# Gate products by seven block products for half of the row tiles, and branch rounds in another order

## The chip, the cores and the metric

One Trainium2 chip, one of its cores. The metric is device time in microseconds (us) of one execution, lower is better. Engines: TensorE (PE) for matmuls, VectorE (DVE), ScalarE (ACT), GpSimd (POOL), and SyncE (SP), which issues most DMAs; each works through its own list in order, and they meet through semaphores.

## What is computed

One decoder layer on 256 tokens, all in float32 (the reference, cut):

```python
h = rms_norm(x, g_attn[l])
qa, ka, va, fa, qb, kb, vb, ga, gb = jnp.split(h @ w_in[l], offs, axis=-1)
o_a = merge_heads(fox_attention(q_a, k_a, v_a, log_f))          # 8 heads, forgetting
o_b = merge_heads(dilated_attention(q_b, k_b, v_b, slopes))     # 8 heads, dilated
merged = jax.nn.sigmoid(ga) * (o_a @ w_br_fox[l]) + jax.nn.sigmoid(gb) * (o_b @ w_br_dil[l])
x = x + merged @ w_out[l]
u = rms_norm(x, g_ffn[l]) @ w_up[l]        # 2048 -> 2 x 5632, causal conv over 3 tokens
x = x + (jax.nn.silu(gate) * val) @ w_down[l]
```

The width is 2048; the gates ga and gb are 2048 columns each.

## The kernel before

Every product is float32 made of three passes in fp32r: activations and weights are split into a high and a low part, and high x high, high x low and low x high are summed in a PSUM bank. Tokens are two row tiles of 128. A weight tile is 256 rows of the contraction by 512 columns (512 KB). One such tile is a **unit**: ACT writes its high part (`high(n)`, w_hi), DVE its low part (`low(n)`, w_lo), PE runs 2 row tiles x 2 contraction tiles x 3 passes = 12 matmuls over it (`rows_unit`) and counts up `used`. w_hi and w_lo are rings of RING = 6 units: `high(n)` waits for unit n - 6 to be used, so ACT and DVE work up to six units ahead of PE. Raw weights go through 4 slots of `raw` (SP loads a slot again once `low` has read it).

A round is 8 units: one block of 512 columns over all of the contraction. The order is: 12 rounds for queries, keys and values in 4 groups of 4 heads (a slot is a unit's place in its group, 0 to 23); 8 gate rounds (ga and gb by turns for the column blocks c = 0 to 3), each evacuated by ACT with a sigmoid; 4 branch rounds, of which units 0 to 3 are the forgetting half into banks 0 and 1 and units 4 to 7 the dilated half into banks 2 and 3; the output rounds; then the feed-forward part. Attention of a group runs between the units of the next group: scores, softmax on DVE and ACT (`softmax_head`, `exps`), transposes of the probabilities (`copy_pt`), values, and the split of the output (`out_high`, `out_low`) into actB. The last four heads (12 to 15) run between the units of the gate rounds, at u = 1, 4 and 7 of the ga rounds. `fox_part` and `dil_part` multiply branch banks by the gates; the sum in `tmp` is transposed after unit 2 of the next round and split into actA (`merged_high`, `merged_low`, which counts `mt_lo`).

The feed-forward part already multiplies half of the contraction of each pair of up blocks by seven block products instead of eight (P1 to P7). A product unit has one row tile: 6 matmuls. The weights of P7, P6, P5 and P4 are sums of tiles; they are made in place in raw_x and raw_y (two tiles each) by accumulating DMAs that POOL issues (`add_tile`) and by adds on DVE, while SP loads the plain tiles. Sums of banks are made by ACT copies and DVE adds. The order is written out by hand on each engine; waits are on constant counts.

## Time and profile before

| | us |
|---|---|
| median of 3 runs | 1385.45 (1384.43 to 1386.55) |
| the profiled execution, its own time | 1384.28 |
| its span, first to last instruction | 1382.5 |
| PE busy | 1371.6 (99%) |
| DVE, ACT, POOL busy | 969.0, 776.6, 94.7 |
| DMA, whole span | 290.52 MB, 210 GB/s |

An engine's busy time is the union of its instructions. Matmuls overlap in the pipeline, so a matmul's own duration is longer than its spacing. "Idle before" is the time in which the engine waited for the named releaser. The stages in this execution: group 3 of the heads from 241 us, gate rounds 307.0 to 484.7, branch rounds to 575, output rounds and the start of the feed-forward part after that; a steady feed-forward block is 64.4 us, as 755.5 to 819.9.

### The profile page before, as it was taken

To read this page: it belongs to the slowest core of one execution; us is meant where nothing else is said; L and a number is where in the kernel's file an instruction comes from. 1 tells how busy PE (TensorE), PEld (TensorE's weight loads), DVE (VectorE), ACT (ScalarE), POOL (GpSimd) and SP (SyncE) were. 2 spreads that over 40 slices of the span, in tenths; PEclk is the share of its full clock that TensorE was granted. 3 is DMA by queue.
4 is the path that set the end of the run, shared out by engine and by line. 5 is a ranking of instruction groups with operands and counts; after the bars stand their busy time and mean duration, and the time that the engine had idled before them with its cause. 6 is when DMAs were issued, how large, how long until landed. Compare 5 with 4: busy or idle time off the path is not lost.

```text
span 1382.5 us, 16197 instructions
## 1 busy us (share of the span) xinstructions
PE 1371.6 (99%) x6241; PEld 1136.2 (82%) x6241; DVE 969.0 (70%) x1196; ACT 776.6 (56%) x963; POOL 94.7 (7%) x115
## 2 busy tenths in 40 slices
PE   9999999999999999999989999999999999999999
PEld 7888888888888888888878888888888888888887
DVE  5646555665554456657688979788878888797975
ACT  6655455454545444446675656565665666565652
POOL 0101011100000000001010101010010101010100
PEclk9999999999999999999999999999999999999999
DMA  9765555556666555667898787696878787878741
GB/s 337 242 207 170 171 168 168 175 165 185 181 192 186 187 192 183 218 226 220 272 245 264 206 249 229 197 267 181 270 182 286 170 290 181 267 203 248 224 139 61
DMA packets 112189, 290.52 MB, mean 210 GB/s; under 512 B 11368, under 2 KB 12656, under 8 KB 111600
## 3 DMA queue, kind: packets, MB, share of 16 engines
q1 hardware_dynamic: 98528, 250.83, 54.3%
q0 software_dynamic: 9504, 34.61, 14.0%
q10 hardware_dynamic: 4080, 4.05, 0.9%
q8 instruction: 49, 0.80, 0.2%
q14 instruction: 28, 0.23, 0.1%
HBM read 287.34 MB, written 2.11 MB: 209 GB/s over the span
## 4 chain that ended last, share of the span: by engine, by line
PE 97%; DMA 1%; DVE 1%; ACT 0%; issue 0%; SPq 0%; POOL 0%; ACTq 0%
PE acc L430 21%; PE acc L432 20%; PE acc L431 20%; PE acc L448 6%; PE acc L452 6%; PE acc L450 6%; PE acc L463 5%; PE acc L467 5%; PE acc L465 5%; PE acc L654 1%; DMA raw_y<-w_up 1%; PE acc L488 1%; PE acc L476 1%; PE acc L496 1%; PE acc L509 0%; DVE w_lo L1111 0%
## 5 line engine op out<-in xcount | busy, mean ns | idle before, releaser
L1111 DVE TENSOR_TENSOR w_lo<-raw,w_hi 128x1024 fp32r<-128x1024 f32 x291 | 354.0, 1224 | 267.5 <-ACT w_hi L791 265.3
L791 ACT ACTIVATE w_hi<-raw 128x1024 fp32r<-128x1024 f32 x291 | 307.4, 1059 | 318.8 <-PE acc L432 272.3
L430 PE MATMUL acc<-w_hi,actA 128*128 128x512 f32 x1116 | 442.4, 396 | 1.4 <-DVE w_lo L1111 1.4
L432 PE MATMUL acc<-w_hi,actA 128*128 128x512 f32 x1116 | 435.1, 390 | 0.0
L431 PE MATMUL acc<-w_lo,actA 128*128 128x512 f32 x1116 | 434.4, 389 | 0.0
L432 PEld LDWEIGHTS acc<-w_hi,actA 128*128 128x128 f32 x1116 | 209.5, 188 | 44.5
L430 PEld LDWEIGHTS acc<-w_hi,actA 128*128 128x128 f32 x1116 | 209.7, 188 | 43.7 <-issue 2.0
L431 PEld LDWEIGHTS acc<-w_lo,actA 128*128 128x128 f32 x1116 | 209.8, 188 | 41.9
L448 PE MATMUL acc<-w_hi,actB 128*128 128x512 f32 x352 | 137.1, 390 | 0.0
L452 PE MATMUL acc<-w_hi,actB 128*128 128x512 f32 x352 | 137.0, 389 | 0.0
L450 PE MATMUL acc<-w_lo,actB 128*128 128x512 f32 x352 | 136.9, 389 | 0.0
L791 ACT ACTIVATE w_hi<-raw_y 128x1024 fp32r<-128x1024 f32 x88 | 93.2, 1060 | 68.7 <-PE acc L432 32.4
L1111 DVE TENSOR_TENSOR w_lo<-raw_y,w_hi 128x1024 fp32r<-128x1024 f32 x88 | 107.3, 1222 | 31.9 <-ACT w_hi L791 31.8
L791 ACT ACTIVATE w_hi<-raw_x 128x1024 fp32r<-128x1024 f32 x66 | 70.0, 1061 | 53.7 <-PE acc L452 32.6
L1111 DVE TENSOR_TENSOR w_lo<-raw_x,w_hi 128x1024 fp32r<-128x1024 f32 x66 | 78.9, 1219 | 9.0 <-ACT w_hi L791 9.0
L1542 POOL DMA_DIRECT2D raw_y<-w_up x44 | 38.4, 872 | 642.1 <-DVE w_lo L1111 598.8
L452 PEld LDWEIGHTS acc<-w_hi,actB 128*128 128x128 f32 x352 | 66.1, 188 | 13.9
L450 PEld LDWEIGHTS acc<-w_lo,actB 128*128 128x128 f32 x352 | 66.1, 188 | 13.8
L448 PEld LDWEIGHTS acc<-w_hi,actB 128*128 128x128 f32 x352 | 66.1, 188 | 13.7
L1371 DVE SCALAR_TENSOR_TENSOR work<-acc,smalls_sb,work 128x255 f32<-128x255 f32 (+1 forms) x176 | 72.5, 474 | 0.6 <-ACT work L1008 0.6
L463 PE MATMUL acc<-w_hi,actB 128*128 128x512 f32 x176 | 69.4, 394 | 0.0
L1404 DVE TENSOR_TENSOR work<-acc,work 128x512 f32<-128x512 f32 x88 | 56.6, 684 | 17.6 <-PE acc L432 17.6
(179 smaller groups left out, 1579.5 us busy)
## 6 DMA issues: line engine op xcount, KB each, us to landing
raw<-w_in SPq DMA_DIRECT2D x159, 512.0 KB, 3.8
raw_x<-w_up SPq DMA_DIRECT2D x44, 512.0 KB, 5.0
raw_y<-w_up POOLq DMA_DIRECT2D x44, 512.0 KB, 7.9
raw<-w_up SPq DMA_DIRECT2D x38, 512.0 KB, 4.6
raw<-w_down SPq DMA_DIRECT2D x34, 512.0 KB, 5.0
raw<-w_out SPq DMA_DIRECT2D x28, 512.0 KB, 4.1
raw_y<-w_up SPq DMA_DIRECT2D x22, 512.0 KB, 4.2
raw_x<-w_up POOLq DMA_DIRECT2D x22, 512.0 KB, 5.5
```

The lines of the kernel that those rows point to most:

```text
L430: nc.tensor.matmul(o, lhsT=a_h, rhs=w_hi[:, s, k, :], start=first and k == 0, stop=False)
L431: nc.tensor.matmul(o, lhsT=a_h, rhs=w_lo[:, s, k, :], start=False, stop=False)
L432: mm = nc.tensor.matmul(o, lhsT=a_l, rhs=w_hi[:, s, k, :], start=False, stop=last and k == KU - 1)
L448: nc.tensor.matmul(o, lhsT=a_h, rhs=w_hi[:, s, k, :], start=False, stop=False, skip_group_check=True)
L450: nc.tensor.matmul(o, lhsT=a_h, rhs=w_lo[:, s, k, :], start=False, stop=False, skip_group_check=True)
L452: mm = nc.tensor.matmul(o, lhsT=a_l, rhs=w_hi[:, s, k, :], start=False, stop=kt == KT - 1, skip_group_check=True)
L463: nc.tensor.matmul(o, lhsT=a_h, rhs=w_hi[:, s, k, :], start=first and kt == 0, stop=False, skip_group_check=True)
L465: nc.tensor.matmul(o, lhsT=a_h, rhs=w_lo[:, s, k, :], start=False, stop=False, skip_group_check=True)
L467: mm = nc.tensor.matmul(o, lhsT=a_l, rhs=w_hi[:, s, k, :], start=False, stop=kt == HK - 1, skip_group_check=True)
L791: nc.scalar.activation(w_hi[:, n % RING, :, :], src.rearrange("p (k n) -> p k n", k=KU), ACT.Copy).then_inc(hi_done, 1)
L1111: nc.vector.tensor_tensor(w_lo[:, n % RING, :, :], src.rearrange("p (k n) -> p k n", k=KU), w_hi[:, n % RING, :, :].bitcast(f32), ALU.subt ...
L1371: t = nc.vector.scalar_tensor_tensor(out=conv[:, j, lag:SEQ], in0=bank[(4, 7)[j // 2]][:, (j % 2) * SEQ:(j % 2 + 1) * SEQ - lag], scalar=s ...
```

## The change

For each column block c the ga and gb rounds are done together. The first 1024 of the 2048 rows of the contraction are done by seven products (P3, P1, P7, P6, P5, P2, P4, each 2 units of 6 matmuls), the other 1024 in the plain form (4 units for ga, 4 for gb, 12 matmuls each), in the order of `gate_units`. The four quarters of the activations are rebuilt from their high and low parts by DVE in slots 8 to 11 of group 3 (`quarters`), their differences formed in slots 12 to 15 and split by ACT (slots 14, 16, 17, 19, 20) and DVE (18 to 21). The parts of P3, P5 and P6 lie in actB[10:16], so the outputs of heads 10 and 11 are kept in `kept` and split later (`kept_lo`). The weights' sums are made in raw_x and raw_y as in the up blocks: POOL's accumulating DMA after P3's split (into raw_y) and after P7's t2 add (into raw_x), DVE adds after P7 (t2) and P2 (t4); there is no accumulate for P4. ACT copies bank 0 after P1, P6, P5 and the last plain unit, DVE adds banks 7, first, 3, second and 7 again into ga and gb; the sigmoids follow in place, two wide ones for each c, those of c during block c + 1, the last in branch round 0. The four gate banks are given out by `gate_banks`.

The branch rounds have 4 units each: the four forgetting ones first, then the four dilated ones; banks (1, 3) and (0, 2) by turns. Heads 12 to 15 move from the gate rounds to the forgetting rounds: scores after unit 0, transposes of the probabilities after unit 3, values after unit 0 of the next round (head 15: of the first dilated round). The merged block is transposed after unit 2 of the next dilated round. Output rounds use banks (6, 7), (1, 3), (0, 2); in the first feed-forward block it is P1 that waits for x2_done 3, where the next output unit did. On SP the raw_x and raw_y loads of the gates stand between the plain ones; on POOL prepare_dil of heads 13 to 15 comes after the gates' accumulates.

```diff
+
+        units += product("P3") + plain(0, 0) + product("P1") + plain(0, 1) + product("P7")
+        units += product("P6") + plain(0, 2) + product("P5") + plain(0, 3) + plain(1, 0)
+        units += product("P2") + plain(1, 1) + product("P4") + plain(1, 2) + plain(1, 3)
...
+
+OUT_BANKS = ((6, 7), (1, 3), (0, 2))
 
 
 def ffn_units():
...
+        def gate_part(name, kt):
+            if name in GATE_PARTS:
+                part = parts_g[:, GATE_PARTS.index(name), kt, :]
+                return part[:, 0:P], part[:, P:2 * P]
+            at, r = {"P1": (kt, 0), "P7": (kt, 1), "P2": (HK + kt, 0), "P4": (HK + kt, 1)}[name]
+            return actA[:, at, r * P:r * P + P], actA[:, at, SEQ + r * P:SEQ + r * P + P]
...
+                    continue
+                _, c, name, q = unit
+                if name == "P5":
+                    sp.wait_ge(lo_done, n)
+                    load_gate_b21(c, q)
+                elif name == "P2" and c < 3:
+                    sp.wait_ge(t4_added, QU * c + q + 1)
+                    load_gate_b11(c + 1, q)
+                elif name == "P4" and c < 3:
+                    sp.wait_ge(lo_done, n)
+                    load_gate_b22(c + 1, q)
...
+            def gate_product(n, c, name, q):
+
+                first_bank, second_bank = gate_banks(c)
+                if q == 0:
+                    if c == 0:
+                        pe.wait_ge(h_part_lo, 4 if name == "P7" else 3)
+                        pe.wait_ge(h_part_hi, 3 if name == "P3" else 6)
+                    if name == "P3" and c:
+                        pe.wait_ge(g_c11, c)
+                    elif name == "P1" and c:
+                        pe.wait_ge(g_u1, c)
+                    elif name == "P7" and c:
+                        pe.wait_ge(g_c22, c)
+                        pe.wait_ge(g_c21, c)
+                    elif name == "P7":
+                        pe.wait_ge(qkt_done, 4 * GROUPS)
+                    elif name == "P6":
+                        pe.wait_ge(g_p1, c + 1)
+                    elif name == "P5":
+                        pe.wait_ge(g_v, c + 1)
+                o = bank[{"P3": second_bank, "P1": 0, "P7": 7, "P6": 0, "P5": 0, "P2": first_bank, "P4": 3}[name]]
+                pe.wait_ge(lo_done, n)
+                s = n % RING
...
+            def gate_plain(n, c, side, j):
+
+                first_bank, second_bank = gate_banks(c)
+                if side == 0 and j == 0 and c:
+                    pe.wait_ge(g_c12, c)
+                    pe.wait_ge(g_c21, c)
+                elif side == 0 and j == 0:
+                    pe.wait_ge(act_evac, 4)
+                pe.wait_ge(lo_done, n)
+                s = n % RING
+                for r, o in enumerate((bank[second_bank], bank[0]) if side else (bank[first_bank], bank[3])):
+                    if side and r and j == 0:
+                        pe.wait_ge(g_u0, c + 1)
...
-                for m in range(2):
-                    R = GATE0 + m + 2 * c
-                    pe.wait_ge(act_evac, 3 + m + 2 * c)
-                    for u in range(UPR):
-                        rows_unit(UPR * R + u, actA, (KU * u, KU * u + 1), bank[2 * m:2 * m + 2], u == 0, u == UPR - 1)
-                        if m == 0 and u == 1:
-                            attend_scores(q_of(3)[:, c, :], lambda a, b: k_of(3)[:, c, a:b])
-                        elif m == 0 and u == 4:
-                            attend_transpose(12 + c)
-                        elif m == 0 and u == 7:
-                            v = v_of(3)
-                            attend_values(12 + c, v[:, 0, c * P:(c + 1) * P], v[:, 1, c * P:(c + 1) * P])
...
+                if c == 0:
+                    pe.wait_ge(g_c11, 4)
+                    pe.wait_ge(g_c21, 4)
+                elif c == 1:
+                    pe.wait_ge(g_u1, 4)
+                    pe.wait_ge(g_c12, 4)
+                else:
+                    pe.wait_ge(fox_merged, c - 1)
+                for u in range(4):
+                    branch_unit(c, u)
+                    if u == 0:
+                        if c:
+                            last_values(c - 1)
+                        attend_scores(q_of(3)[:, c, :], lambda a, b: k_of(3)[:, c, a:b])
+                    elif u == 3:
+                        attend_transpose(12 + c)
...
                 if c == 0:
-                    pe.wait_ge(fox_merged, 4)
+                    pe.wait_ge(g_c22, 4)
                     pe.wait_ge(mt_lo, 6)
                 elif c == 1:
...
+                        if g == 3 and slot in (14, 16, 17):
+                            name = {14: "P5", 16: "P6", 17: "P3"}[slot]
+                            act.wait_ge(h_made, {"P5": 5, "P6": 7, "P3": 8}[name])
+                            nc.scalar.activation(parts_g[:, GATE_PARTS.index(name), :, 0:P],
+                                                 h_of[{"P5": 2, "P6": 0, "P3": 3}[name]], ACT.Copy)\
+                                .then_inc(h_part_hi, 1)
...
+                if unit == ("H", c, "P1", QU - 1):
+                    act.wait_ge(used, n + 1)
+                    nc.scalar.activation(ga[:, 0, to], bank[0], ACT.Copy, scale=-1.0).then_inc(g_p1, 1)
+                elif unit == ("H", c, "P6", QU - 1):
+                    act.wait_ge(used, n + 1)
+                    nc.scalar.activation(ga[:, 1, to], bank[0], ACT.Copy, scale=-1.0).then_inc(g_v, 1)
+                elif unit == ("H", c, "P5", QU - 1):
+                    act.wait_ge(used, n + 1)
+                    if c == 0:
+                        act.wait_ge(h_part_lo, 4)
+                    nc.scalar.activation(gb[:, 0, to], bank[0], ACT.Copy).then_inc(g_u0, 1)
+                elif unit == ("G", c, 1, PLAIN - 1):
+                    act.wait_ge(used, n + 1)
+                    if c == 3:
+                        act.wait_ge(kept_lo, 1)
+                    nc.scalar.activation(gb[:, 1, to], bank[0], ACT.Copy).then_inc(g_u1, 1)
...
+            def gate_sigmoid(c):
+                act.wait_ge(g_c11, c + 1)
+                act.wait_ge(g_c12, c + 1)
+                act.wait_ge(g_c21, c + 1)
+                act.wait_ge(g_c22, c + 1)
+                for r in range(RT):
+                    both = work_rows[:, :, r, c * NB:(c + 1) * NB]
+                    nc.scalar.activation(both, both, ACT.Sigmoid, scale=xrs[:, r:r + 1]).then_inc(g_sig, 1)
...
+                for u in range(4):
+                    high(BR_UNIT + 4 * c + u + RING)
+                    if u == 0:
+                        if c:
+                            out_high(12 + c - 1)
+                        exps(12 + c)
+                    elif u == 1 and c == 0:
+                        gate_sigmoid(3)
+                    elif u == 3:
+                        copy_pt(12 + c)
...
+            def gate_bank_sums(n, unit):
+
+                c = unit[1]
+                first_bank, second_bank = gate_banks(c)
+                to = slice(c * NB, c * NB + NB)
+                if unit == ("H", c, "P3", 0) and c:
+                    before = slice(c * NB - NB, c * NB)
+                    dve.wait_ge(g_u1, c)
+                    gate_rest(gb[:, 1, before])
+                elif unit == ("G", c, 0, 2):
+                    dve.wait_ge(g_v, c + 1)
+                    gate_result(bank[7], ga[:, 1, to], g_v7)
+                elif unit == ("H", c, "P2", QU - 1):
+                    dve.wait_ge(used, n + 1)
+                    dve.wait_ge(g_p1, c + 1)
+                    gate_result(bank[first_bank], ga[:, 0, to], g_c11)
+                elif unit == ("H", c, "P4", QU - 1):
+                    dve.wait_ge(used, n + 1)
+                    dve.wait_ge(g_v7, c + 1)
+                    gate_result(bank[3], ga[:, 1, to], g_c21)
+                elif unit == ("G", c, 1, PLAIN - 1):
+                    dve.wait_ge(used, n + 1)
+                    dve.wait_ge(g_u0, c + 1)
+                    gate_result(bank[second_bank], gb[:, 0, to], g_c12)
...
             def fox_part(c):
-                dve.wait_ge(used, UPR * (BR0 + c) + 4)
+                dve.wait_ge(used, BR_UNIT + 4 * c + 4)
+                dve.wait_ge(g_sig, 2 * c + 2)
                 for r in range(RT):
-                    t = nc.vector.tensor_tensor(tmp[:, r, :], bank[r][:, :], ga[:, r, c * NB:(c + 1) * NB], ALU.mult)
+                    part = ga[:, r, c * NB:(c + 1) * NB]
+                    t = nc.vector.tensor_tensor(part, bank[br_banks(c)[r]], part, ALU.mult)
...
+            for n, unit in enumerate(GATES, GATE_UNIT):
+                _, c, kind, q = unit
+                if kind == "P3":
+                    pool.wait_ge(lo_done, n)
+                    add_gate_tile(c, q, raw_y[:, q, :], y_summed[q])
+                elif kind == "P7":
+                    pool.wait_ge(t2_added, QU * c + q + 1)
+                    add_gate_tile(c, q, raw_x[:, q, :], x_summed[q])
             for c in range(1, 4):
```

## Rows read from the trace of the kernel before

**Rows 1.** The page: busy us, share of span, count; granted clock in tenths by 40 slices.

```profile
PE 1371.6 (99%) x6241; PEld 1136.2 (82%) x6241; DVE 969.0 (70%) x1196; ACT 776.6 (56%) x963; POOL 94.7 (7%) x115
PEclk9999999999999999999999999999999999999999
```

**Rows 2.** Waits of PE: engine, line waited for, us in total, times, longest.

```profile
PE acc L654 <- DVE tmp L1414: 3.0, 1, 3.0
PE acc L463 <- ACT tmp L1038: 1.5, 1, 1.5
```

**Rows 3.** Windows: busy us and count by engine, clock, DMA share, GB/s.

```profile
core 0: us, PE busy (x) PEld busy (x) DVE busy (x) ACT busy (x) POOL busy (x), PEclk, DMA share, GB/s
...
307.00:484.70 177.70, 177.70 (x799) 147.41 (x798) 88.48 (x111) 89.51 (x108) 3.04 (x6) 1.00 0.63 186
...
755.50:819.90 64.40, 64.40 (x293) 53.48 (x292) 54.02 (x64) 39.57 (x44) 5.23 (x7) 1.00 0.79 229
```

**Rows 4.** PE's timeline in a gate round: start, duration, two units' first matmuls.

```profile
339.28 0.39 PE L430 MATMUL acc<-w_hi,actA 128*128 128x512 f32 x1
...
342.00 0.39 PE L430 MATMUL acc<-w_hi,actA 128*128 128x512 f32 x1
```

**Rows 5.** Timelines of ACT and DVE there: one unit's high and low part.

```profile
343.62 1.06 ACT L791 ACTIVATE w_hi<-raw 128x1024 fp32r<-128x1024 f32 x1 [1.66 <-PE acc L432]
...
344.71 1.23 DVE L1111 TENSOR_TENSOR w_lo<-raw,w_hi 128x1024 fp32r<-128x1024 f32 x1 [1.50 <-ACT w_hi L791]
```

**Rows 6.** DVE's timeline in a steady feed-forward block: bank sums; t2 add.

```profile
828.04 1.29 DVE L1404 TENSOR_TENSOR work<-acc,work 128x512 f32<-128x512 f32 x2 [0.34 <-PE acc L432]
...
834.54 1.22 DVE L1115 TENSOR_TENSOR raw_y<-raw_y,raw_x 128x1024 f32<-128x1024 f32 x1
```

**Rows 7.** POOL's accumulates issued in 690:700, 730:760 and 760:790: issue to landing.

```profile
DMA to landing us min/median/max: 9.4/10.7/12.0
...
DMA to landing us min/median/max: 5.4/5.4/5.5
...
DMA to landing us min/median/max: 5.4/7.1/10.9
```

**Rows 8.** The page's DMA issues: count, KB each, median us to landing.

```profile
raw<-w_in SPq DMA_DIRECT2D x159, 512.0 KB, 3.8
raw_x<-w_up SPq DMA_DIRECT2D x44, 512.0 KB, 5.0
...
raw_y<-w_up SPq DMA_DIRECT2D x22, 512.0 KB, 4.2
```

**Rows 9.** DMA queues in 307:484, then in 719:1300: packets, MB, share.

```profile
q1 hardware_dynamic: 17002, 32.79, 62.2%
...
q1 hardware_dynamic: 28288, 103.04, 50.4%
q0 software_dynamic: 7980, 29.06, 28.1%
```

**Rows 10.** POOL's timeline: prepare_dil of head 12.

```profile
294.05 0.83 POOL L1506 TENSOR_TENSOR softmax<-consts_sb,st 128x384 f32<-128x384 f32 x1
```

**Rows 11.** A head's softmax on DVE, and the table loads that ACT does.

```profile
356.73 0.55 DVE L1123 TENSOR_TENSOR softmax<-acc,softmax 128x384 f32<-128x384 f32 x1
...
360.07 0.55 DVE L1147 TENSOR_SCALAR softmax<-softmax,st 128x128 f32<-128x128 f32 x2
...
373.21 1.28 ACT L969 ACT_TABLE_LOAD   x1
374.51 1.27 ACT L969 ACTIVATE work<-acc,st 128x512 f32<-128x512 f32 x2
```

**Rows 12.** Branch round 1 on PE and DVE: transposes of the merged block, their split.

```profile
514.46 1.03 PE L476 MATMUL acc<-smalls_sb,tmp 128*128 128x128 f32 x8
515.25 0.48 PE L430 MATMUL acc<-w_hi,actB 128*128 128x512 f32 x1
...
515.81 1.23 DVE L1111 TENSOR_TENSOR w_lo<-raw,w_hi 128x1024 fp32r<-128x1024 f32 x1 [1.20 <-ACT w_hi L791]
...
520.56 1.28 DVE L1159 TENSOR_TENSOR actA<-acc,actA 128x512 fp32r<-128x512 f32 x2
```

More of the change, by code:

```diff
@@ new lines, in _, with branch_unit @@
+            pe.wait_ge(qn_done, 2 * GROUPS)
+            for n, unit in enumerate(GATES, GATE_UNIT):
+                if unit[0] == "H":
+                    gate_product(n, unit[1], unit[2], unit[3])
+                else:
+                    gate_plain(n, unit[1], unit[2], unit[3])
+            def branch_unit(m, u):
+                pair = [bank[b] for b in br_banks(m)]
+                kt = KU * u if m < 4 else KT // 2 + KU * u
+                rows_unit(BR_UNIT + 4 * m + u, actB, (kt, kt + 1), pair, u == 0, u == 3)
@@ L806, in out_high @@
                 act.wait_ge(o_ready, h + 1)
-                nc.scalar.activation(actB[:, h, 0:SEQ], bank[6][:, 0:SEQ], ACT.Copy).then_inc(o_hi, 1)
+                if h in (10, 11):
+                    nc.scalar.activation(kept[:, h - 10, :], bank[6][:, 0:SEQ], ACT.Copy).then_inc(o_lo, 1)
+                else:
+                    nc.scalar.activation(actB[:, h, 0:SEQ], bank[6][:, 0:SEQ], ACT.Copy).then_inc(o_hi, 1)
             def merged_high(c):
@@ L974, in _, with gate_sum @@
-            for c in range(4):
-                for u in range(UPR):
-                    high(UPR * (BR0 + c) + u + RING)
-                    if c and u == 2:
+            def gate_sum(n, unit):
+                c = unit[1]
[16 more added lines that the diff above has]
+                    nc.scalar.activation(gb[:, 1, to], bank[0], ACT.Copy).then_inc(g_u1, 1)
@@ new lines, in gate_sigmoid @@
+            def gate_sigmoid(c):
[6 more added lines that the diff above has]
+                    nc.scalar.activation(both, both, ACT.Sigmoid, scale=xrs[:, r:r + 1]).then_inc(g_sig, 1)
+            for n, unit in enumerate(GATES, GATE_UNIT):
+                gate_sum(n, unit)
+                high(n + RING)
+                _, c, kind, j = unit
+                if unit == ("G", c, 0, 1):
+                    if c:
+                        gate_sigmoid(c - 1)
+                    if c == 3:
+                        act.wait_ge(used, GATE_UNIT + GATES.index(("H", 3, "P3", QU - 1)) + 1)
+                        nc.scalar.activation(actB[:, 10:12, 0:SEQ], kept, ACT.Copy).then_inc(kept_hi, 1)
@@ L1249, in _ @@
                             softmax_head(h, prep, g == 3)
-                        elif g > 0 and at == 5:
+                        elif g > 0 and at == 5 and h < 10:
                             out_low(h)
+                        if g == 3:
+                            quarters(slot)
                         if u == (UPR - 1 if R else UPR - 2) and m < 2:
@@ L1315, in _ @@
+                nc.vector.tensor_tensor(tmp[:, :, :], ga[:, :, c * NB:(c + 1) * NB], gb[:, :, c * NB:(c + 1) * NB],
+                                        ALU.add).then_inc(merged, 1)
             for c in range(4):
-                for u in range(UPR):
-                    low(UPR * (BR0 + c) + u + RING)
+                for u in range(4):
+                    if c == 0 and u == 0:
+                        dve.wait_ge(g_u1, 4)
+                        gate_rest(gb[:, 1, 3 * NB:4 * NB])
+                    elif u == 3:
+                        fox_part(c)
+                    low(BR_UNIT + 4 * c + u + RING)
+                    if u == 0:
+                        if c:
+                            out_low(12 + c - 1)
+                        dve.wait_ge(prep_ready, prepared(12 + c))
+                        softmax_head(12 + c, prep, True)
@@ L1318, in _ @@
+            for c in range(4):
+                for u in range(4):
                     if u == 3:
@@ L1321, in _ @@
                             dve.wait_ge(mt_ready, 2 * c)
-                        else:
-                            dve.wait_ge(act_evac, 4 + 8)
-                        fox_part(c)
-                dil_part(c)
+                        dil_part(c)
+                    low(BR_UNIT + 16 + 4 * c + u + RING)
+                    if c == 0 and u == 0:
+                        out_low(15)
             def add_x2(n, c, banks):
```

326 lines of the change are left out of this document (244 added, 82 removed).

## Prediction, made before the change was run

> **What bounds the kernel now.** I read the page first, then the waits of PE, then the windows by stage, and only then single rows. The page shows TensorE busy for 1371.6 of 1382.5 us at the full granted clock of 2.4 GHz, with no slice below it [rows 1]. PE's waits say where it was not busy: besides the first microseconds, 3.0 and 1.5 us in the first feed-forward block [rows 2], and nothing in the stages that this change touches. In the gates' stage (307.0 to 484.7 us) PE is busy for the whole of its 177.7 us while DVE is busy for 88.5, ACT for 89.5 and the DMA engines at 0.63 [rows 3]. So PE is the bound there, and only matmuls less, or a new wait on PE, move the end.
>
> **What one matmul costs.** A matmul's row says 0.39 us, but that is latency in a pipeline. Two first matmuls of following units start at 339.28 and 342.00 us, twelve matmuls apart [rows 4]: 2.72 / 12 = 0.2267 us each. It is the same in product units: a feed-forward block issues 276 long matmuls and 16 transposes (two groups of some 0.9 us) and takes 64.4 us [rows 3]; 276 x 0.2267 = 62.6. A change of weights or bank costs no extra. So a plain unit (two row tiles) takes 2.72 us and a product unit (one row tile of products, 6 matmuls) 1.36.
>
> **1. Gates by seven products.** Before: 4 column blocks x 2 gates x 8 units x 12 = 768 matmuls. After, for each c: 7 products x 2 units x 6 = 84, and 8 plain units x 12 = 96, together 180; 720 in all. Removed: 48 x 0.2267 = **10.9 us**, all on the path. A block now takes 180 x 0.2267 = 40.8 us.
>
> **2. What the other engines get for it.** Units grow from 64 to 88. Each is split by ACT (1.06 us) and DVE (1.23 us), and DVE's comes out about 2.35 us after ACT may start [rows 5]. For each block DVE has 22 x 1.23 = 27.1, four adds of whole tiles (t2, t4) at 1.22 = 4.9, five sums out of banks at 0.64 = 3.2 [rows 6]: 35.2 of 40.8 us. ACT has 22 x 1.06, four copies of a bank (0.6 each) and two wide sigmoids (1.1 each): 28. Both fit, DVE at 86%. They run six units ahead of PE, so what is late in a stretch of products (1.36 us a unit on PE, 2.45 on DVE for P7 with its add) is caught up in plain units (2.72). Cost taken: nothing. If that cover were gone, DVE's 35.2 us still lies under 40.8.
>
> The PE waits on banks are each covered by work in between: P6 after P1's copy by one plain and two product units (5.4 us against 0.6), P5 after P6's by one plain unit (2.7 against 0.6), the second row tile of G10 after P5's by 4.1, the next block's P1 after the last copy by 5.4. Where they are thinnest, 2 us remain.
>
> **3. The loop through the buffers.** raw_x and raw_y go round: P3 split, accumulate (D), P7 split, t2, accumulate (D), P5 split, load into raw_x, P2 split, t4, P4 split, load into raw_y, next P3. In numbers: five splits of 2.35, two adds of 1.25, 2.5 of queue on DVE and ACT before P4 (its neighbours' splits, t4 of the other half and P5's copy), loads of 5.0 and 4.2 [rows 8], so 25.95 + 2D. POOL's accumulates land 5.4 to 5.5 us after issue when two are alone, up to 10.9 when four queue up in one product stretch, and 9.4 and 12.0 beside SP's burst of loads in the first block [rows 7]. The gates queue never more than two and have no such burst. With D = 5.5 the loop is 36.95 us, under the block's 40.8, and PE waits for nothing; it closes at D = 7.4. Walking the units one by one, the split of the tightest ones (P5, P6, P7) ends 5 us before PE comes to them, so a late transfer first eats 5 us. With three returns the stall is about 3 x (2D - 14.9) - 5 us: none to D = 8.2, 7 at 9.5, 10.4 at 10, 22 at 12.
>
> What D is for w_in no row shows: its rows are 2 KB, those of w_up here 4 KB. From above: a software packet takes 28.1% x 16 x 581 / 7980 = 0.33 us in the feed-forward stage [rows 9]; an accumulate of w_up is 145 packets, 2.9 us of all engines. A tile of w_in is some 274 packets; if each still took 0.33, that were 5.6 us and D 8.2 alone, 12 for the second of a pair. From below: plain loads of w_in take 62.2% x 16 x 177 / 17002 = 0.104 us a packet against 50.4% x 16 x 581 / 28288 = 0.166 for w_up, so half the row is nearly half the time (18% more by the byte), and land after 3.8 us, not later than w_up's [rows 8, 9]. That excludes a gain but gives D = 5.4 to 6. I take 6, since the plain loads are the same rows of the same tensor; both ends stay in the range. The engines' load goes from 0.63 to about (14 x 1.77 + 4 x 3.4) / 40.8 = 0.94 by the packets' times under light load, 0.85 if they shorten as in other full stretches: high, so D is the weak number.
>
> The Trainium skill (DMA: Bandwidth & Descriptors, "Why small descriptors are slow") gives a fixed cost of about 3 cycles per packet beside one cycle per 32 bytes. By that, 2 KB rows would cost 2% more than 4 KB rows, not the 18% that the queue's rows show here; D would be 5.5 and the sum the same.
>
> **4. First block and the quarters.** In group 3 DVE gets 12 operations of about 0.65 and ACT six of 0.6 (four quarters rebuilt, four differences, splits). DVE is busy 0.6 of the time in that stage and idles 1.5 us in most slots [rows 5], so they go into gaps. PE's P3 needs those of slot 20, ready more than 5 us before. POOL's first accumulate stands behind prepare_dil(12), which ends at 294.9 us [rows 10]; it lands by 302 to 307, P7's split could start at 308.4. Nothing.
>
> **5. Last four heads in the forgetting rounds.** The attention matmuls and transposes are as many as before: 0. Their chain gets tighter, 4 units a round. Scores to normalised took 356.73 to 360.6 us = 3.9 [rows 11], 2.3 after the unit's end; with out_low (0.4) before it, ready 6.7 us after the unit that issues the scores, against three units = 8.2 until the transposes. DVE per round: 4 x 1.23 + 3.9 + 0.4 + 1.3 (fox_part) = 10.5 of 11.8. The one tight place is round 0: ACT has gate_sigmoid(3) between exps(12) and copy_pt(12): a table load of 1.28 [rows 11] and 2.1 of sigmoid, then two late splits. By addition copy_pt is ready 11.75 us after the first unit; PE wants it at 4 x 2.72 + 0.8 = 11.7. Cost: 0 to 0.3.
>
> The rows show one table load, 1.28 us, and the next activation starts 0.01 after it. The Trainium skill (ScalarE: Activation LUTs, "What ACT_TABLE_LOAD costs") adds a drain to about 2.66 us a switch; the rows do not show it. With it round 0 would wait 1.4 us more.
>
> **6. Dilated rounds of 4 units.** Transposes after unit 2 now leave one unit (2.72) before the output rounds ask for mt_lo 6. From the transposes' start DVE's split ends at +2.6 (517.04 against 514.46), merged_low adds 1.28: +3.75 with the semaphore; PE gets there at 0.8 + 2.72 = +3.5 [rows 12]. Cost 0.2 to 0.3. dil_part (2.5 us) has 8 us until the next transposes, kept and o_lo 16 have 5 us of cover for 3. Their banks alternate: nothing. The feed-forward stage is untouched; I leave its 4.5 us of waits [rows 2] where they are.
>
> **Sum.** -10.9 + 0.3 + 0.2 = -10.4. The profiled execution took 1384.28 us (its span 1382.5 and 1.8 around it): 1373.9. The median of the runs is 1.17 above it, so 1385.45 - 10.4 = **1375.1 us**.
>
> **Rivals.** *A: the loop bites in part.* D between 8.2 and 9.5: PE waits 0 to 7 us in the gates, each at a P5 or P7; 1376 to 1382, say 1379. For it: the packets' 0.33 us and the load near 0.9. Against: two accumulates alone land in 5.5. The same figure stands for small waits of some 4 us in the branch rounds.
> *B: the loop takes all the gain.* D of 9.5 to 10.1 gives 1383 to 1386.
> *C, the other side: the accumulates decide.* If a pair of 2 KB accumulates lands after 11 us (the packet's price kept, the second behind the first), the loop is 48 us, the gates' stage waits 3 x 7.1 - 5 = 16 us, and the time is 1385.45 - 10.4 + 16 = 1391. It is slower from D = 10.1 on.
> *D: no fewer matmuls on the path, because DVE (35 of 41 us) bounds the products.* It would need 5.6 us more of DVE work for each block; every item above is counted, so I see it only together with A.
> *E: the feed-forward start shifts.* Its 4.5 us of waits hang on two DMA landings; they may shrink or grow by 2: 1373 to 1377.
>
> **Chances.** Forecast with E (1373 to 1377.5) 0.66; A 0.16; B 0.10; C 0.08. Range: 1372.5 (the feed-forward start loses some wait) to 1384.0 (into B), 0.85 or so by these cases. Under 0.2% (2.8 us) no measurement of this kernel tells a change from none. Faster by more: 0.66 + 0.16 = 0.82; within: 0.10; slower: 0.08.
>
> **What would show it.** The long matmuls must fall by 48 (about 6241 to 6193 instructions), the stretch from the gates' first to last matmul from 177.7 us to some 163, since 3.6 us of attention moves out too. Landings of raw_x and raw_y from w_in: 5.4 to 7 us right, above 8 wrong. ACT's waits for raw_x may appear, PE's should not. At the first output round a PE wait of 0.3 behind merged_low; in the second forgetting round none above 0.5 on prob_t. The forecast is wrong if PE shows waits over 3 us in all between 307 and 640.

## The result, and the profile after

The changed kernel takes **1376.72 us**, the median of its runs (1376.06 to 1378.59), beside 1385.62 for the kernel before on the same chip: a ratio of 0.9938, 95% interval 0.9921 to 0.9956. That is 8.9 us, where 10.4 were forecast. Its profiled execution took 1376.06 us and its span is 1374.3, 8.2 below the span of before. The page's first line, busy us, share of span and count:

```profile
PE 1361.5 (99%) x6193; PEld 1127.2 (82%) x6193; DVE 1033.3 (75%) x1267; ACT 804.4 (59%) x999; POOL 114.2 (8%) x131
```

TensorE has 6193 instructions against 6241 [rows 1], just the 48 that were to go, and its granted clock is 2.4 GHz in every slice as before. The waits of PE come next, to be read against [rows 2]: engine, line waited for, us in total, times, longest.

```profile
PE acc L858 <- DVE tmp L1779: 3.3, 1, 3.3
PE acc L588 <- ACT tmp L1313: 1.5, 1, 1.5
...
PE acc L745 <- ACT work L1204: 1.1, 1, 1.1
```

The first two are the feed-forward start, as before. L745 is new: the first matmul of a gate product waits for L1204, ACT's copy of bank 0 after P6. (The view puts down 1.1 of what the starts of the matmuls below give as 1.28.) The gates' stretch (windows: busy us and count by engine, clock, DMA share, GB/s) is 163.0 us long, as forecast, and PE is not busy for 1.3 of it, where before it was busy without a break [rows 3]:

```profile
303.40:466.40 163.00, 161.74 (x713) 133.27 (x712) 133.12 (x122) 105.01 (x114) 16.79 (x14) 1.00 0.80 218
```

A listing of where two long matmuls of PE's timeline start further apart than 0.2267 us shows smaller waits too. Behind attention's small matmuls it has 0.08 to 0.19 in either kernel, which were there before. New in the changed stages are three places (start of the matmul before, start of the late one, the excess):

```
363.27 L774 -> 364.78 L745 1.28    P5 of block 1
446.31 L774 -> 446.83 L745 0.29    P5 of block 3
565.20 L557 -> 565.69 L555 0.26    first output round
```

With the matmul after each, which comes 0.1 late as well (0.11, 0.11, 0.08), that is 2.1 us. The feed-forward start waits 0.3 to 0.4 longer. 10.9 - 2.1 - 0.4 = 8.4, and the spans differ by 8.2: the account closes.

The last thing that the prediction asked for are the landings. POOL's accumulates issued in 339.5 to 342 (second into raw_y), 350 to 352 and 352 to 354 (both into raw_x), issue to landing:

```profile
DMA to landing us min/median/max: 5.9/7.2/8.5
...
DMA to landing us min/median/max: 6.1/6.1/6.1
...
DMA to landing us min/median/max: 6.2/6.2/6.2
```

The first of these windows holds both accumulates of the raw_y pair: 5.9 is the first and 8.5 the second. D is 6 for three of a block's four accumulates and 8.5 for the fourth (8.4 to 8.7 in blocks 1 to 3, and 9.4 in block 0).

### The profile page after: what moved, and what is told of

Same layout as the page of the kernel before. It is cut to its first block, busy times and chain, and to the rows that moved or that the text cites. A ratio compares the mean times of both kernels' runs of the same rounds, so it can differ in the third digit from the quotient of the medians.

```text
span 1374.3 us, 16297 instructions
## 1 busy us (share of the span) xinstructions
PE 1361.5 (99%) x6193; PEld 1127.2 (82%) x6193; DVE 1033.3 (75%) x1267; ACT 804.4 (59%) x999; POOL 114.2 (8%) x131
## 4 chain that ended last, share of the span: by engine, by line
PE 96%; DMA 1%; ACT 1%; DVE 1%; issue 1%; SPq 0%; POOL 0%; ACTq 0%
PE acc L555 16%; PE acc L557 16%; PE acc L556 16%; PE acc L577 6%; PE acc L573 6%; PE acc L575 6%; PE acc L588 5%; PE acc L592 5%; PE acc L590 5%; PE acc L772 2%; PE acc L774 2%; PE acc L770 2%; PE acc L745 2%; PE acc L747 2%; PE acc L749 2%; PE acc L858 1%
## 5 line engine op out<-in xcount | busy, mean ns | idle before, releaser
L1389 DVE TENSOR_TENSOR w_lo<-raw,w_hi 128x1024 fp32r<-128x1024 f32 x259 | 314.4, 1223 | 165.9 <-ACT w_hi L1013 163.2
L1013 ACT ACTIVATE w_hi<-raw 128x1024 fp32r<-128x1024 f32 x259 | 273.0, 1058 | 227.3 <-PE acc L557 169.9
L555 PE MATMUL acc<-w_hi,actA 128*128 128x512 f32 x860 | 341.6, 397 | 1.6 <-DVE w_lo L1389 1.5
L557 PE MATMUL acc<-w_hi,actA 128*128 128x512 f32 x860 | 335.8, 390 | 0.0
L556 PE MATMUL acc<-w_lo,actA 128*128 128x512 f32 x860 | 335.1, 390 | 0.0
L555 PEld LDWEIGHTS acc<-w_hi,actA 128*128 128x128 f32 x860 | 161.7, 188 | 34.4 <-issue 2.6
L557 PEld LDWEIGHTS acc<-w_hi,actA 128*128 128x128 f32 x860 | 161.5, 188 | 34.3
L556 PEld LDWEIGHTS acc<-w_lo,actA 128*128 128x128 f32 x860 | 161.8, 188 | 32.3
L1013 ACT ACTIVATE w_hi<-raw_y 128x1024 fp32r<-128x1024 f32 x120 | 127.0, 1060 | 97.0 <-PE acc L557 35.6
L1389 DVE TENSOR_TENSOR w_lo<-raw_y,w_hi 128x1024 fp32r<-128x1024 f32 x120 | 146.1, 1222 | 41.1 <-ACT w_hi L1013 40.5
L1013 ACT ACTIVATE w_hi<-raw_x 128x1024 fp32r<-128x1024 f32 x90 | 95.3, 1059 | 72.4 <-PE acc L577 32.6
L1389 DVE TENSOR_TENSOR w_lo<-raw_x,w_hi 128x1024 fp32r<-128x1024 f32 x90 | 108.2, 1222 | 24.1 <-ACT w_hi L1013 24.0
```

The costliest lines, as they stand in the source:

```text
L555: nc.tensor.matmul(o, lhsT=a_h, rhs=w_hi[:, s, k, :], start=first and k == 0, stop=False)
L556: nc.tensor.matmul(o, lhsT=a_h, rhs=w_lo[:, s, k, :], start=False, stop=False)
L557: mm = nc.tensor.matmul(o, lhsT=a_l, rhs=w_hi[:, s, k, :], start=False, stop=last and k == KU - 1)
L1013: nc.scalar.activation(w_hi[:, n % RING, :, :], src.rearrange("p (k n) -> p k n", k=KU), ACT.Copy).then_inc(hi_done, 1)
L1389: nc.vector.tensor_tensor(w_lo[:, n % RING, :, :], src.rearrange("p (k n) -> p k n", k=KU), w_hi[:, n % RING, :, :].bitcast(f32), ALU.subt ...
```

## Why ACT is late at P5

ACT's timeline in block 1 shows what stands ahead of the copy (start, duration; in brackets the idle time before and its releaser):

```profile
353.85 0.57 ACT L1201 ACTIVATE work<-acc 128x512 f32<-128x512 f32 x1
354.32 1.05 ACT L1013 ACTIVATE w_hi<-raw 128x1024 fp32r<-128x1024 f32 x1
356.84 1.06 ACT L1013 ACTIVATE w_hi<-raw_x 128x1024 fp32r<-128x1024 f32 x1 [1.47 <-DMA raw_x<-w_in]
357.92 1.28 ACT L1223 ACT_TABLE_LOAD   x1
359.21 2.19 ACT L1223 ACTIVATE work<-work,st 128x1024 f32<-128x1024 f32 x2
361.31 1.04 ACT L1013 ACTIVATE w_hi<-raw_x 128x1024 fp32r<-128x1024 f32 x1
362.26 1.99 ACT L1013 ACTIVATE w_hi<-raw 128x1024 fp32r<-128x1024 f32 x2
364.16 0.57 ACT L1204 ACTIVATE work<-acc 128x512 f32<-128x512 f32 x1
```

PE's own row at the end of it:

```profile
364.78 0.50 PE L745 MATMUL acc<-w_hi,actB 128*128 128x512 f32 x1 [1.13 <-ACT work L1204]
```

P6's last matmul starts at 360.55, so bank 0 could be copied from about 361. ACT reaches the copy at 364.16, since its list is in order: the two splits of P5's tiles, which wait for the accumulates into raw_x, the sigmoids of block 0 between them, in this block with a table load of 1.28, and then two more splits, all stand before it. PE has one plain unit (2.72) in that time and then waits. In block 2 the same copy ends at 405.6 and P5 starts at 405.7; in block 0, which has no sigmoids to do, it ends at 321.7 and P5 starts a microsecond later. The **queue theory** is that these waits come from ACT's order. The **transfer theory**, its rival, is that they come from the loop through raw_x and raw_y (rival A of the prediction), whose landings are what ACT waits for at 356.84.

## Experiments

Plain units are named by their gate and number: G00 to G03 are the four of ga, G10 to G13 the four of gb.

**The table load, ahead of its time.** A one-column sigmoid in block 0 makes ACT load the table where it has time.

```diff
+                if unit == ("G", 0, 1, 1):
+                    nc.scalar.activation(st[:, 90:91], st[:, 91:92], ACT.Sigmoid)
```

> One tiny sigmoid on ACT in the first gate block (after G11) brings the table load there, where ACT has time; nothing else changes. Theory Q (queue on ACT): in the changed kernel the copy of P6's bank in block 1 stood behind a late split of raw_x (1.47 us for the DMA), a table load (1.28) and two sigmoids (2.19), and PE waited 1.28 us for it before P5. Without the table load the copy starts 1.28 earlier and PE's wait there is 0.0 to 0.1; the wait of 0.3 in block 3 stays; time 1.4 us less than the changed kernel. Rival T (transfers): the wait follows from the late landing of raw_x; then it stays at 1.3 us. Rival B (bank or weights): the same.

Measured: 1374.94 us, ratio 0.9925 (0.9905 to 0.9945), span 1372.5. PE's wait of block 1 is gone, that of block 3 stays:

```profile
PE acc L745 <- ACT work L1204: 0.2, 1, 0.2
```

No transfer was touched and 1.28 us of ACT's list was enough to remove the largest wait. That speaks for the queue theory.

**The sigmoids after the copy.** Those of block c - 1 come after unit G11 of block c.

```diff
+                if unit == ("G", c, 1, 1) and c:
+                    gate_sigmoid(c - 1)
                 if unit == ("G", c, 0, 1):
-                    if c:
-                        gate_sigmoid(c - 1)
```

> The two sigmoids of block c - 1 come after G11 instead of after G01 of block c; the copy of kept stays where it was. Theory Q: both PE waits on ACT's bank copies (1.28 us in block 1, 0.3 in block 3) go, none takes their place, since after G11 ACT has four units until its next copy: 1.8 us less. Theory T: the waits stay. If ACT's late splits matter for PE by themselves, new waits of PE on w_lo would show after G11.

Measured: 1375.67 us, ratio 0.9931 (0.9911 to 0.9950), span 1373.4. No wait on L1204 is left, but a new one on DVE's sum of a bank has come:

```profile
PE acc L770 <- DVE work L1611: 0.6, 2, 0.4
```

The listing has it as 0.60 at 388.4 and 0.36 at 430.0, at the first plain units of blocks 2 and 3. Late in block 1 the table load and the sigmoids (379.16 to 382.6) now stand ahead of a split on ACT; DVE idles 3.23 us for that split, and its bank sum at 387.64, for which block 2 waits, stands behind it. The wait was moved, not removed.

**The removed matmuls put back.** Twelve matmuls more for each block, inside P4's units and into bank 4, which nobody reads.

```diff
+                    if name == "P4":
+                        for w in (w_hi, w_lo, w_hi):
+                            nc.tensor.matmul(bank[4], lhsT=a_h, rhs=w[:, s, k, :], start=True, stop=True)
```

> The changed kernel with 12 more matmuls in each gate block (in P4's units, high and low weights into a bank that nothing reads): as many long matmuls as before the change. If the gain is nothing but the 48 matmuls at 0.2267 us, this gives 10.9 us back less the 1.3 us of PE waits that the longer blocks hide: about 1386 us, 0.5 to 1 above the kernel before. If part of the gain came from elsewhere (the order of the branch rounds, fewer bank changes), the time stays clearly under the kernel before.

Measured: 1387.54 us, ratio 1.0013 (1.0004 to 1.0023), with 6241 instructions on PE. That is 10.8 us above the changed kernel, so the 48 matmuls are worth what [rows 4] said, and everything else in the change costs 1.9 us. The waits of blocks 1 and 3 stayed (1.08 and 0.32), where they were expected to be hidden. Each block has 2.7 us more here for its loop. So the waits are set within a block, from P3 to P5, and not by the loop around it.

**The transfers, held back.** Two small POOL operations stand ahead of each accumulate of a gates' tile, each waited for.

```diff
             def add_gate_tile(c, q, to, done):
+                for _ in range(2):
+                    nc.gpsimd.tensor_tensor(consts_sb[:, 0:256], smalls_sb[:, 0:256], smalls_sb[:, 0:256],
+                                            ALU.add).then_inc(idled, 1)
+                    idles[0] += 1
+                    pool.wait_ge(idled, idles[0])
```

> Two small operations on POOL (about 0.8 us each) stand ahead of every accumulate of the gates: each lands 1.6 us later, the second of a pair about 2.0. Loop theory (P3 back to P3 through raw_x and raw_y in 25.95 us and two accumulates, against a block of 40.8): the second of a pair already has 8.5 + 6.0 = 14.5, so 14.5 + 4 - 14.9 = 3.6 us over for each of three returns, less 5 us of lead: PE waits 6 us more. Lead theory (each transfer is covered by its own six units, nothing adds up): P7's cover is 17 us, P5's 11.7, so no wait on the splits at all; only the wait for P6's copy in blocks 1 to 3 grows by up to 1.6 each.

Measured: 1404.69 us, ratio 1.0140 (1.0120 to 1.0160), 28 us above the changed kernel. Both numbers missed, for one reason first: the delay was not what was planned. POOL's timeline (two operations in the rows of L1908):

```profile
357.93 3.10 POOL L1908 TENSOR_TENSOR consts_sb<-smalls_sb 128x256 f32<-128x256 f32 x2 [6.61 <-DVE raw_y L1398]
361.32 1.19 POOL L1913 DMA_DIRECT2D raw_x<-w_in  x1 [0.30 <-POOL consts_sb L1908]
362.10 3.71 POOL L1908 TENSOR_TENSOR consts_sb<-smalls_sb 128x256 f32<-128x256 f32 x2
```

The pair took 1.3 to 1.6 us four times of sixteen, and 2.2 to 3.7 the other twelve, among them all that came right behind an accumulate's issue. Measured from the end of PE's unit before P5, the second accumulate into raw_x was issued 4 to 6 us later than in the changed kernel, and PE waited 5.0 to 6.0 in each block:

```profile
PE acc L745 <- ACT work L1204: 15.6, 3, 5.8
PE acc L745 <- DVE w_lo L1389: 5.0, 1, 5.0
```

These waits are 21.3 us in the listing. Most of what is left of the 28 is a lower granted clock behind each of them: the next long matmuls start 0.43 us apart instead of 0.23 in each of the four blocks, some 7 us in all.

**The same, with a bank of its own for P5.** If ACT's copy is all that PE waits for, P5 in bank 5 needs no copy ahead of it. The second row tile of gb's plain units goes to bank 5 with it. In this kernel P5's bank holds no P1 + P6, so that term is missing in gb: it serves for the time alone.

```diff
-"P6": 0, "P5": 0,
+"P6": 0, "P5": 5,
...
-                    elif name == "P5":
-                        pe.wait_ge(g_v, c + 1)
+                    elif name == "P5" and c:
+                        pe.wait_ge(g_u1, c)
```

> The delayed kernel (e5) with P5 and the second row tile of the gb units in bank 5, which is idle in this stage, in place of bank 0 on top of P1 and P6. So P5 no longer waits for ACT's copy of P6's bank; the term P1 + P6 is missing in gb. In e5 PE waited 5.1 to 5.8 us in each block for that copy. Queue theory: the copy stands on ACT behind the splits of P5, and the second of these waits for the accumulate into raw_x, so an accumulate is covered only up to that copy. Then the waits on the copy go and what is left is P5's own second tile: it lands at 372.1 in block 1 of e5, is split by 374.5, and PE wants it at 372.3, so 2.2 us for each block, on w_lo; about 13 us less than e5, 1391 us. Loop theory: the time lost is that of the ring of buffers; then the 5 us for each block stay and only change their name to w_lo: 1404.

Measured: 1404.11 us, ratio 1.0135 (1.0117 to 1.0154).

```profile
PE acc L745 <- DVE w_lo L1389: 17.8, 4, 4.9
```

The waits stayed, 3.8 us in block 0 and 4.5 to 5.1 in the others, and changed their name, to the split of P5's own tile. With transfers as late as this, the transfer theory holds: the copy was only the first of two things that were late together.

**Transfers made shorter.** The gates' weights laid out in advance as tiles with 4 KB rows, for SP's loads as for POOL's accumulates (the latter shown).

```diff
-                nc.gpsimd.dma_start(to.rearrange("p (k n) -> p k n", k=KU),
-                                    w_in_v[:, KU * q:KU * q + KU, col:col + NB], accum_op=ALU.add).then_inc(done, 16)
+                nc.gpsimd.dma_start(to, w_gate[1, c, q, :, :], accum_op=ALU.add).then_inc(done, 16)
```

> The changed kernel with the gates' weights laid out in tiles in memory, like w_up's: 4 KB rows in place of 2 KB in all gate loads and accumulates; same bytes. If the row length sets the accumulate (my price by the byte: 18%), a single one lands after 5.4 to 5.5 us in place of 6.0, and POOL's issue takes 0.87 in place of 1.20. The wait of 1.28 us for P6's copy in block 1 falls by 0.6 to 0.9, the small one in block 3 goes: 1 us less than the changed kernel. If row length does not matter, all stay.

Measured: 1376.79 us, ratio 0.9936 (0.9923 to 0.9950): no gain, where 1 us was expected. The accumulates into raw_x of block 1:

```profile
DMA to landing us min/median/max: 5.5/5.5/5.5
...
DMA to landing us min/median/max: 5.7/5.7/5.7
```

That is 0.5 us less than with 2 KB rows, and the wait of block 1 fell from 1.28 to 0.72. The wait of block 3 rose from 0.29 to 1.28: there the accumulates issued at 432.96 and 435.35 took 7.0 us each. Why that pair was late is open. So the wait at P5 does follow the landing ahead of it, in both directions, as long as ACT's order leaves nothing in hand; the length of the rows alone doesn't settle it.

**ACT's order mended.** The sigmoids stand at unit G03, behind P6's copy but not as late as G11; the table is loaded in block 0; the output rounds wait for `mt_lo` in steps.

```diff
-                if unit == ("G", c, 0, 1):
+                if unit == ("G", c, 0, 3):
                     if c:
                         gate_sigmoid(c - 1)
+                    else:
+                        nc.scalar.activation(st[:, 90:91], st[:, 91:92], ACT.Sigmoid)
...
-                    pe.wait_ge(mt_lo, 6)
+                    pe.wait_ge(mt_lo, 4)
...
-                    if c == 0 and u == 6:
-                        pe.wait_ge(mt_lo, 8)
+                    if c == 0 and u in (4, 6):
+                        pe.wait_ge(mt_lo, u + 2)
```

> The changed kernel with the sigmoids of block c - 1 after G03 of block c (behind P5's splits, with four wide units ahead), one tiny sigmoid at G03 of block 0 for the table load, and the first output round waiting for mt_lo 4, 6 and 8 at units 0, 4 and 6. Queue theory: the waits of 1.28 and 0.3 us on ACT's copies and the 0.3 us at the output round go, no new ones above 0.3 us: 1374.7 us. If the sigmoids only hand the delay on, as after G11 (0.6 and 0.4 us on DVE's sum of bank c12), 1375.5.

Measured: **1374.41 us**, ratio 0.9919 (0.9905 to 0.9932), span 1372.3: the lowest median here, though not clear of the 1374.94 with the table load alone. The window of the gates' stage has PE busy throughout, and the listing has no place from 290 to 620 but those behind attention's small matmuls:

```profile
303.40:466.40 163.00, 163.00 (x721) 134.99 (x721) 134.71 (x123) 105.88 (x115) 16.79 (x14) 1.00 0.80 221
```

So all of the new waits were waits on ACT's and PE's order, at the transfers as they are. Behind the first output round the mended kernel is 2.3 us ahead of the changed one, of which the removed waits are 2.1. That the spans differ by 2.0 is partly chance: at the feed-forward start two waits are 0.4 and 0.7 us shorter in the mended kernel's execution, but behind the first of them eight spacings of matmuls, from 705.3 on, are 0.43 instead of 0.23 us, a lower granted clock that costs 1.6.

**Mended, with 4 KB rows.**

> e8 with the 4 KB rows of e7. If accumulates no longer touch PE in e8, this equals e8 within 0.5 us; if it is faster by 1 us or more, the transfers still cost something that no PE wait shows.

Measured: 1374.61 us, ratio 0.9921 (0.9908 to 0.9935). With no wait left, shorter transfers bring nothing.

**How far are the transfers from deciding?** The last two kernels have one POOL operation instead of two ahead of each accumulate, in the order of the changed kernel and in the mended one.

> The changed kernel with one small POOL operation (128x256, waited for) ahead of each accumulate of a gates' tile. From the rows of the run with two such operations a pair took 1.3 us when POOL was idle before and 3.1 to 3.7 us right behind an accumulate's issue, so one operation is taken as 0.7 to 1.7 us: the first accumulate of each pair is issued about 0.9 us later, the second about 2 us later. Queue theory (P6's copy stands on ACT behind splits that wait for raw_x, with no slack left in blocks 1 and 3): every delay of raw_x goes straight to PE there, so the waits grow by about 2 us in blocks 1 and 3 and some 1 us in blocks 0 and 2: about +5 us, 1381 to 1383. Theory that the transfers have room and only the table load made the waits: under +2 us, 1377 to 1378.5.

> The same one POOL operation ahead of each accumulate, in the mended order (sigmoids of block c - 1 after unit G03 of block c, table loaded early, output rounds waiting in steps for mt_lo). Queue theory with the prediction's loop (25.95 + 2D against 40.8, plus 5 us of units in hand): the second of each pair adds about 2 us to D on each of the two laps, D about 8, 41.9 us against 40.8, 3 x 1.1 - 5 below zero: no stall, 1374 to 1375.5, and the difference to the same delay in the unmended order is 6 to 8 us. Theory that the chain of transfers itself is at its limit already (as the two operations' 5 us in each block, left in place with the free bank, could be read): the delays show as waits whatever ACT's order, 1379 to 1384, within 3 us of the unmended order.

Measured: 1385.21 us, ratio 0.9998 (0.9989 to 1.0007), and 1384.56, ratio 0.9993 (0.9983 to 1.0004). In the order of the changed kernel both theories missed, with 1381 to 1383 and 1377 to 1378.5: PE waits 0.94, 1.89, 2.92 and 1.92 at P5 of the four blocks. The mended order saves 0.65 us here, which is within the noise, not 6 to 8: the queue theory missed and the transfer theory's 1379 to 1384 was nearly met. The delay counts on two of a block's four accumulates, by some 2 us each, and takes the whole gain. The chain of waits of the mended kernel with the delay shows the loop, one lap from t4 to t4 (start, us, what):

```profile
326.12 1.22 DVE raw_y L1396
...
330.34 2.28 DVE w_lo L1392 x2
332.64 5.48 DMA raw_y<-w_in
338.14 1.07 ACT w_hi L1013
339.23 1.24 DVE w_lo L1392
340.55 0.61 POOL consts_sb L1911
341.45 1.20 POOL raw_y L1916
342.65 1.21 POOL consts_sb L1911
344.14 8.98 DMA raw_y<-w_in
353.15 1.07 ACT w_hi L1013
354.24 1.24 DVE w_lo L1392
355.50 1.24 DVE raw_y L1401
356.81 1.53 POOL consts_sb L1911
358.63 5.69 DMA raw_x<-w_in
364.34 1.07 ACT w_hi L1013
365.43 4.64 DVE w_lo L1392 x4
370.09 1.23 DVE raw_y L1396
```

The lap is 370.09 - 326.12 = 43.97 us, and the next one, to 414.44, is 44.35. PE isn't in it: it is bound by this chain alone. From the end of the first tile's split to the second accumulate's issue it has 344.14 - 340.47 = 3.67 us on the first half of the lap, where the mended kernel without the delay has 1.4 to 1.8, and on the second, from the end of t2, 358.63 - 356.73 = 1.90, where that has 0.3: the delay adds 3.5 to 3.9, say 3.7. Without it the lap would be **40.3 us**, against the 40.8 that PE needs for a block. This is an estimate by subtraction, good to some 0.2: the reserve is about half a microsecond.

The waits of PE in that kernel:

```profile
PE acc L745 <- ACT work L1204: 7.3, 3, 3.0
...
PE acc L745 <- DVE w_lo L1392: 0.9, 1, 0.9
```

They are 8.9 us in the listing (1.08, 3.16, 1.82, 2.80 in the four blocks), while the span is 13.4 longer than that of the mended kernel. What comes on top is the clock. After the wait of 3.0 us PE's rows are twice as far apart for nine matmuls:

```profile
367.83 0.54 PE L745 MATMUL acc<-w_hi,actB 128*128 128x512 f32 x1 [3.00 <-ACT work L1204]
...
368.60 0.63 PE L749 MATMUL acc<-w_hi,actB 128*128 128x512 f32 x1
369.02 0.63 PE L745 MATMUL acc<-w_hi,actB 128*128 128x512 f32 x1
...
371.57 0.39 PE L745 MATMUL acc<-w_hi,actB 128*128 128x512 f32 x1
...
372.03 0.40 PE L749 MATMUL acc<-w_hi,actB 128*128 128x512 f32 x1
```

From 368.60 to 369.02 are 0.42 us, from 371.57 to 372.03 two spacings of 0.23: the one is 1.2 GHz, the other 2.4. Behind the waits of 3.16 and 2.80 there are eight such spacings each, 1.6 and 1.5 us more, and none behind those of 1.08 and 1.82. 8.9 + 3.1 and 0.1 for the matmul behind each wait are 12.4, and the kernel is 12.7 behind the mended one at the gates' end. The other 0.6 come at the feed-forward start, whose wait on ACT is 1.5 here and 0.8 there; 0.3 are not accounted for.

The length of the wait doesn't say whether the clock falls. In the unmended order with the same delay it fell behind the waits of 2.92 and 1.92 and not behind 1.89. At the feed-forward start PE waits 2.8 to 3.3 us in every kernel: the clock fell behind it in the mended one (705.3) and in both with one delay, and not in the changed one, whose wait of 3.3 is the longest, nor in the kernel before with its 3.0. What decides is open.

## The prediction, point by point

**The matmuls (part 1): right.** 48 fewer, and 10.8 us when they were put back, against 10.9.

**Engines and copies (part 2): the step that failed.** DVE and ACT fit as said (133.1 and 105.0 of 163.0 us). But "P5 after P6's by one plain unit (2.7 against 0.6)" took the copy as ready 0.6 after the bank is. The plain unit had to cover ACT's list ahead of the copy too: from P6's end at about 361 there are 3.2 us of sigmoid and three splits, and then 0.6, and they are that late because a table load of 1.28 and the landing at 356.84 stand before them. The forecast said that 2 us remain where the cover is thinnest; what remained was 1 us in block 0, 0.1 in block 2, -0.3 in block 3 and -1.3 in block 1. All items that stand in that list were in the prediction (the sigmoids in part 2's count, the table load in [rows 11]), and in part 5 they were laid end to end for branch round 0. They weren't for the copies. Size: 1.8 of the 2.1 us.

**The loop (part 3): formula right, D too small.** The prediction took 25.95 + 2D with D = 6, 37.95 us, 2.85 under the block. The second accumulate into raw_y decides, with 8.4 to 9.0 behind block 0, and the second into raw_x has 5.7 to 6.4. By the prediction's own sign, 5.4 to 7 right and above 8 wrong, D = 6 was wrong for one accumulate in four. By the formula that is 25.95 + 14.6 = 40.55; the chain gave 40.3. So the terms other than D were right within 0.3 in their sum, D was 7.3 in the mean of the deciding two, and the point at which the loop closes, D = 7.4, was nearly reached. Rival C was therefore much nearer than the text had it: from D = 7.3 and not 6, and a delay of 3.7 us on the lap was enough to take the whole gain. The 5 us in hand was wrong as well: with a lap of 44.2 the forecast's stall is 3 x 3.4 - 5 = 5 us, and 8.9 came, so about 1.3 were in hand. And a stall of 2 to 3 us in one place can have a price that the text left out, the lower clock behind it: some 1.5 us each time that it came.

The [rows 9] estimate of 0.33 us for a packet whatever its size is refuted. The queues of the changed kernel in 303 to 447 us:

```profile
q1 hardware_dynamic: 12427, 23.95, 50.2%
q0 software_dynamic: 3898, 7.49, 31.7%
```

31.7% x 16 x 144 / 3898 = 0.19 us for a software packet of half the row. The choice of D near the plain loads' ratio was right for an accumulate that is alone (6.0 against 5.5 with 4 KB rows, 9% more). What it missed is the second of a pair. [rows 7] had shown landings of 7.1 in the median and 10.9 at most where accumulates follow one another closely, and the text kept them for four in a row. The DMA engines' load, put at 0.94 or 0.85, was 0.80.

**Quarters (part 4), heads (part 5): right.** No PE wait from 290 us to the first block's end, none on the probabilities. In branch round 0 ACT did what was added up: table load, sigmoids, two late splits, copy.

```profile
477.37 1.28 ACT L1223 ACT_TABLE_LOAD   x1
478.67 2.19 ACT L1223 ACTIVATE work<-work,st 128x1024 f32<-128x1024 f32 x2
480.76 1.99 ACT L1013 ACTIVATE w_hi<-raw 128x1024 fp32r<-128x1024 f32 x2
482.66 0.46 ACT L1025 ACTIVATE softmax<-acc 128x384 f32<-128x384 f32 x1
```

The activation starts 1.30 after the load does, here and in block 1. The 2.66 us a switch that the Trainium skill states (ScalarE: Activation LUTs, "What ACT_TABLE_LOAD costs") would have put some 1.3 us of wait here, by an estimate with its drain: the copy ends at 483.1 and PE loads the first tile of it at 483.2. No wait is there, so the measurement decides for 1.3 us a switch.

**First output round (part 6): right.** 0.26, where 0.2 to 0.3 was said, behind merged_low:

```profile
564.31 1.28 DVE L1442 TENSOR_TENSOR actA<-acc,actA 128x512 fp32r<-128x512 f32 x2
```

**The sum.** -10.9 + 0.2 + 0.3 was forecast. -10.9 + 1.8 (the copies) + 0.3 (output round) + 0.4 (feed-forward start, rival E's sign) came. The time, 1376.7, lies in the forecast's own range, 1373 to 1377.5. That the loop cost nothing was in part luck: the text had 2.85 us in reserve and the kernel has about 0.5. None of the rivals took place, though a small wait at P5 is where rival A had put one, from another cause.

## What to carry to other kernels

When a bank or buffer is freed by an engine that works in order, its cover has to hold all that stands ahead of the freeing instruction in that engine's list, and the transfers those wait for, not only the instruction's own time. For a loop through buffers, take the landing of the last transfer of a group and compare the lap with the block: a kernel with no wait in its profile may be half a microsecond from being bound by that loop. Delay the transfer a little on purpose and the chain of waits prints the lap.

## What was not expected of the hardware

- The same small POOL operation (128x256) takes 0.60 us in some places and 1.5 to 1.7 in others. In the mended kernel with the delay it took 1.1 to 1.6 each time right behind the issue of an accumulate, and on a POOL that had been idle 0.60 five times and 1.5 to 1.7 five times. What decides is open. Two of them, planned as 1.6 us, took up to 3.7.
- In blocks 1 to 3 of the changed kernel the second of two accumulates of 512 KB lands 8.4 to 8.7 us after its issue where they are issued 1.4 us apart (raw_y), and 6.0 to 6.4 where they are 2.4 us apart (raw_x). The distance isn't all: 2.7 us apart it was 8.98 in the mended kernel with the delay, and with the sigmoids after G11 a pair 1.3 us apart had 7.35.
- POOL's issue of one accumulate takes 1.20 us with 2 KB rows and 0.87 with 4 KB rows; the landing in block 1 (raw_x) is 6.1 to 6.2 against 5.5 to 5.7.
- TensorE's granted clock fell to 1.2 GHz for eight spacings of matmuls behind some waits (3.16, 2.92, 2.80 and 1.92 us) and not behind others (3.3, 3.0 and 1.89): the same wait at the feed-forward start has it in one kernel's execution and not in another's.
